# Reordering the row dots and the route scatters inside the expert stage of a hybrid decoder step

## The reference

```python
def peer_ffn(h, w_q, subkeys, u, v):
    q = (xt @ w_q).reshape(n, PEER_HEADS, 2, PEER_HALF)
    s = jnp.einsum('nhpd,hpkd->nhpk', q, subkeys)
    s_top, i_top = lax.top_k(s, PEER_TOPK)
    ...
    best, sel = lax.top_k(cand, PEER_TOPK)
    eidx = jnp.take_along_axis(cand_idx, sel, axis=-1)
    gate = jax.nn.softmax(best, axis=-1)
    ...
        a = jax.nn.gelu(jnp.einsum('ted,td->te', u[ib], xb))
        return jnp.einsum('te,ted->td', gb * a, v[ib])
```

## Time and profile before

| What | Value |
|---|---|
| Median of 3 runs | 4431.86 us (4416.49 to 4433.48) |
| The profiled execution, its own time | 4428.74 us |
| Its span, first to last instruction | 4427.1 us |
| Mean granted clock of TensorE | 0.972 |
| PE busy | 4207.2 us, 95% |
| DVE busy | 2647.8 us, 60% |
| POOL busy | 1483.2 us, 34% |
| First matmul of the stage of the change | 1943.7 us |
| Gathers and scatters issued | 2054.8 to 3276.0 us |
| Last dot begins | 3289.3 us |

### The profile page before, as it was taken

The page is one execution under the profiler, slowest core; times in us unless marked ns, Lnnn a source line. Parts: engine busy times, 40 slices in busy tenths (PEclk is TensorE's granted clock), DMA queues, the critical chain, the costliest instruction groups (busy, mean ns, idle before and its releaser), DMA issues. The chain is left out here.

```text
span 4427.1 us, 76388 instructions
## 1 busy us (share of the span) xinstructions
PE 4207.2 (95%) x28752; PEld 4110.5 (93%) x28752; DVE 2647.8 (60%) x3612; ACT 1246.2 (28%) x1625; POOL 1483.2 (34%) x1265
## 2 busy tenths in 40 slices
PE   6999999999897899979999999998889999999997
PEld 6999999999765899979999999998789999999997
DVE  5322211111222552245878999998679988888887
ACT  4211132333222221233332333232223223233232
POOL 1000000000011000001446666666736666566552
PEclk8999999999898999989999999999899999999998
DMA  5822333333477443235778887888899999999996
GB/s 209 309 78 85 111 113 109 105 102 107 158 285 268 150 141 123 70 130 179 257 268 280 292 289 282 300 310 302 314 378 368 357 364 355 361 357 359 360 354 256
DMA packets 282382, 1061.85 MB, mean 240 GB/s; under 512 B 43650, under 2 KB 94082, under 8 KB 228930
## 3 DMA queue, kind: packets, MB, share of 16 engines
q1 hardware_dynamic: 165042, 521.13, 33.4%
q0 software_dynamic: 90576, 499.53, 30.4%
q10 hardware_dynamic: 26624, 39.37, 2.4%
HBM read 977.47 MB, written 81.33 MB: 239 GB/s over the span
## 5 line engine op out<-in xcount | busy, mean ns | idle before, releaser
L145 DVE TENSOR_TENSOR w_lo<-w_raw,w_hi 128x1024 fp32r<-128x1024 f32 x458 | 550.9, 1230 | 840.9 <-ACT w_hi L136 840.7
L136 ACT ACTIVATE w_hi<-w_raw 128x1024 fp32r<-128x1024 f32 x458 | 476.3, 1058 | 1019.7 <-PE acc L173 566.4
L173 PE MATMUL acc<-x_hi,w_hi 128*128 128x288 f32 x2592 | 559.6, 298 | 13.3 <-DVE w_lo L145 9.3
L173 PE MATMUL acc<-x_lo,w_hi 128*128 128x288 f32 x2592 | 558.4, 297 | 0.0
L173 PE MATMUL acc<-x_hi,w_lo 128*128 128x288 f32 x2592 | 558.0, 297 | 0.0
L1572 POOL DMA_INDIRECT routes_scratch<-gate_sums,route x384 | 489.6, 1275 | 144.6 <-issue 115.5
L173 PEld LDWEIGHTS acc<-x_hi,w_hi 128*128 128x128 f32 x2592 | 420.7, 190 | 14.9 <-DVE w_lo L145 9.7
L173 PE MATMUL acc<-h_hi,w_hi_peeru 128*128 128x384 f32 (+1 forms) x1280 | 406.4, 334 | 23.5 <-DVE w_lo_peeru L145 23.5
L173 PEld LDWEIGHTS acc<-x_lo,w_hi 128*128 128x128 f32 x2592 | 420.6, 190 | 0.0
L173 PEld LDWEIGHTS acc<-x_hi,w_lo 128*128 128x128 f32 x2592 | 420.4, 190 | 0.0
L173 PE MATMUL acc<-h_hi,w_hi 128*128 128x384 f32 (+1 forms) x1280 | 401.1, 330 | 14.1 <-DVE w_lo L145 14.1
(11 more groups left out here) (340 smaller groups left out, 8302.1 us busy)
## 6 DMA issues: line engine op xcount, KB each, us to landing
w_raw<-in_w_peer_u SPq DMA_DIRECT2D x256, 512.0 KB, 5.2
w_raw<-in_w_peer_v SPq DMA_DIRECT2D x256, 512.0 KB, 6.5
w_raw<-in_w_gate SPq DMA_DIRECT2D x96, 512.0 KB, 3.6
w_raw<-in_w_z SPq DMA_DIRECT2D x66, 512.0 KB, 3.5
k_ring<-in_cache_k SPq DMA_DIRECT2D x64, 512.0 KB, 6.3
v_ring<-in_cache_v POOLq DMA_DIRECT2D x64, 512.0 KB, 6.9
routes_scratch<-zero POOLq DMA_DIRECT2D x8, 3072.0 KB, 46.4
activations_scratch<-a_out ACTq DMA_DIRECT2D x128, 192.0 KB
```

The costliest lines, as they stand in the source:

```text
L136: nc.scalar.activation(slot(q, j)[0], raw[:, j % 4, :], ACT.Copy).then_inc(q["hi"], 1)
L145: nc.vector.tensor_tensor(lo, raw[:, j % 4, :], hi.bitcast(F32), ALU.subtract).then_inc(q["lo"], 1)
L173: last = nc.tensor.matmul(dst, l_, r_[:, cc, c0:c0 + cn], start=(cc == first and p_ == 0), stop=(cc == last_c and p_ == 2))
```

## The change

It edits the two functions that lay out the order. No instruction is added or removed; gathers, scatters and dots change places among the stripes and among each other.

```diff
         def dots_by(s):
 
-            if s < 16:
-                return 0
-            return s - 15 if s <= 34 else min(NGAT, 19 + 7 * (min(s, LAST_FREE) - 34) // 5 + 11 * max(0, s - LAST_FREE) // 5)
+            if s <= 32:
+                return min(24, 3 * max(0, s - 13) // 2)
+            return min(NGAT, 24 + 7 * (min(s, LAST_FREE) - 32) // 5 + 11 * max(0, s - LAST_FREE) // 5)
 
         def scatters_before(q):
 
-            return min(NSCT, 9 * q // 4)
+            return min(NSCT, 9 * q // 4, 48 * (q // 24 + 1))
```

## The result

| | before | changed |
|---|---|---|
| Median | 4432.1 us (4 runs, 4416.5 to 4433.5) | 4528.4 us (4 runs, 4513.6 to 4534.7) |
| Profiled execution, its own time | 4428.7 us | 4534.7 us |

The ratio is 1.0218, 95% interval 1.0189 to 1.0247: **slower by 2.2%, 96 us**. The forecast was 4516 us, slower, with a range up to 4543. Of the 106 us between the two profiled executions, 5.7 lie ahead of the stage (its first matmul starts at 1949.5 us against 1943.7). The stage itself, from its first matmul to its last, grew from 1345.8 to 1445.7 us, by 99.9.

The account below looks back on a forecast made before the run. PE bounds the kernel, losing time where it waits for DVE's weight splits, late when POOL's gathers are. Stalls 109.7 plus slow starts 9.4 give +119, less 34 given back: +85 us on 4431.9, about 4516; range 4474 to 4543.

Parts of the forecast that it names:

- run of 18 (k = 3): 18 scatters in a row before a gather make PE wait for stripe 68: late by 7.1 us.
- run of 24 (k = 4): 24 scatters in a row, priced at 35.6 us, delay the split of stripe 86: late by 11.4 us.
- run of 30 (k = 5): 30 scatters in a row, priced at 42.6 us, delay a split that PE wants: late by 11.5 us.
- run of 36 (k = 6): 36 scatters in a row: PE late by 31.3 us, and 2 more while gathers 146 to 149 come 4.4 us apart.
- run of 42 (k = 7): 42 scatters in a row make PE wait for split 131: late by 46.4 us.
- slow starts: After each of five stalls PE starts at the low clock level, costing 1.9 us each, 9.4 us in all.
- gain in stripes 119 to 143: Outside the bursts, 25 stripes would run at 8.40 us each, 210.0 instead of 242.3 us: 32.3 us given back.
- Covered early runs: Rival, 12%: the bursts k = 3 to 5 cost nothing, as ring and lead hold more than counted: +49 us, 4481.
- A backlog behind a run: Rival, 10%: scatters hold up the gather behind them, so k = 3 to 7 cost 5.6 us more each: 4545 us.
- Free scatters: Rival, 5%: scatters issue so fast that the ring covers the bursts; only the gain of 34 us stays: 4398 us.
- Bursts and gain cancel: Rival, 3%: the bursts cost 34 us in all, as much as is given back: 4432 us.
- Early stripes overfull: Rival, 1%: the 20 us of dots added in stripes 14 to 28 are not hidden by DVE's idle time: 4536 us.

Follow-up runs that it names:

- the even spread: Changed kernel with each head's 48 scatters spread evenly over the gathers until the next head is ready, 1 a gather for the last: 4403.0 us, ratio 0.9940.

## Why the prediction was right

**The mechanism and its places** held: runs of 6 to 42 scatters before gathers 24 to 168, PE's waits at stripes 68, 86/87, 103, 120 and 131, the first two runs covered, no wait in stripes 15 to 32, none at 123 to 130, and 124.8 us of PE waits in the stage where I named "near 120". One sign that I had named for being wrong did show in part: after a run a row landed well under 7.8 us (see below).

**The terms.**

| Term | Forecast | Measured |
|---|---|---|
| run of 18 (k = 3) | 7.1 | 6.7 |
| run of 24 (k = 4) | 11.4 | 5.3 + 5.0 |
| run of 30 (k = 5) | 11.5 | 14.9 |
| run of 36 (k = 6) | 31.3 + 2 | 31.7 + 2.9 |
| run of 42 (k = 7) | 46.4 | 46.7 |
| sum | 109.7 | 113.3 |
| slow starts | 9.4, five stalls | 18.0, eight stalls, 1.4 to 3.1 each; 0.5 more at stripe 115 |
| gain in stripes 119 to 143 | -32.3 | -31.6: they take 299.0 us for 242.2, and 210.6 without the stalls and slow starts (210.0 in the even spread) |
| dot more at stripe 100 | 0 | +2.2 (2.81 for 0.65) |
| dot less at stripe 114 | 0 | -2.3 (8.75 for 11.01) |
| tail behind the last matmul | -2 | 0 |

The slow starts are read by laying the two traces over each other, matmul by matmul, and taking the stall from what each place adds. The measured terms give 113.3 + 18.5 - 31.6 + 2.2 - 2.3 = 100.1; the stage grew by 99.9. So what I missed of the time is the slow starts above all, 9 us. I had taken five where there are eight, each at the 1.9 us of one stall.

Three readings in the prediction are off and change little. Of the 22.7 us that "come after" the 11 us stall, 0.7 come before it, at stripe 101. The run of 24 is priced at 35.6 us; its own rule, 29 us at 1.50 and the rest at 1.28, gives 35.0. And with 1.28 us for every scatter the sum would be some 19 us less, not 14.

**Two errors inside a burst cancelled.** The chain took 7.8 us from a gather's issue to its landing, the median over all gathers. After the five runs even the dot began 5.6 to 6.0 us after the issue (3270.22 to 3275.81 above). The queue had then carried no row for 28 us and more, which is the likely reason; no run tests it by itself. And the runs were slower than I had them: from the first scatter to the gather 28.5, 37.9, 50.0, 51.9 and 56.9 us against 27, 35.6, 42.6, 49.6 and 56. That adds 14.4 us over the five, and the quicker rows take some 10 off: that the stalls came out within 4 us of the forecast is partly luck. The run of 30 is the mis-sized one. It falls on the sums of a head, of which the first two of three instructions have two SBUF inputs, 2.56 us each; under these a scatter takes up to 3.10 us. POOL's timeline of the changed kernel, then DVE's:

```profile
2895.22 3.10 POOL L1572 DMA_INDIRECT routes_scratch<-gate_sums,route  x1 [0.31 <-issue]
2898.62 2.29 POOL L1572 DMA_INDIRECT routes_scratch<-gate_sums,route  x1 [0.30 <-issue]
2901.22 0.97 POOL L1572 DMA_INDIRECT routes_scratch<-gate_sums,route  x1 [0.30 <-issue]
2902.49 0.96 POOL L1572 DMA_INDIRECT routes_scratch<-gate_sums,route  x1 [0.30 <-issue]
2903.76 2.58 POOL L1572 DMA_INDIRECT routes_scratch<-gate_sums,route  x1 [0.30 <-issue]
```

```profile
2894.92 2.55 DVE L1752 TENSOR_TENSOR same_expert<-eid_f,eidx 128x2304 f32<-128x2304 f32 x1
2897.51 2.56 DVE L1754 TENSOR_TENSOR same_expert<-same_expert,gate 128x2304 f32<-128x2304 f32 x1
2900.10 2.55 DVE L1756 TENSOR_REDUCE gate_sum_part<-same_expert 128x48 f32<-128x2304 f32 x1
2902.69 0.21 DVE L1757 TENSOR_TENSOR gate_sums<-gate_sums,gate_sum_part 128x48 f32<-128x48 f32 x1
2902.93 2.56 DVE L1752 TENSOR_TENSOR same_expert<-eid_f,eidx 128x2304 f32<-128x2304 f32 x1
```

The reduction has one input, and the two scatters under it run at 0.97.

**The stage's end.** I credited 2 us because DVE's last dot would no longer trail PE. It now starts at 3363.9 us, 31 us before PE's last matmul ends, yet from the stage's last matmul to the end of the program it is 1138 us in both traces. DVE's last dot wasn't what the end hung on. In both kernels ACT's first split of the next stage comes 3.7 to 3.9 us after ACT issued the store of the last stripe's activations (3290.13 to 3294.06 before, 3395.73 to 3399.39 changed), and ACT's last wait of the stage is for those stores.

**The rivals.** Covered early runs: out, 32 us of stalls there. A backlog behind a run: out, the rows landed sooner. Free scatters: out, 1.28 us each. Bursts and gain cancel: out, the stalls behind the runs alone are 113 us. Early stripes overfull: out, and the kernel with the new dots and no runs says so by itself.

**The Trainium skill.** The Trainium skill, DMA: Bandwidth & Descriptors, section Anatomy of one DMA, gave an estimate of 4.4 us for a row's landing. After a run, from issue to the dot, the trace shows 5.6, so the estimate is nearer to that than to the 7.8 of the median, and still short. The Trainium skill, SBUF — State Buffer, section Who interferes with whom, says that a DVE instruction with two SBUF inputs contends with a GpSimd instruction that reads SBUF. If the issue of a gather or scatter counts as one, the runs agree (1.46, 1.65 and 1.89 us a POOL instruction with none, a third and all of the dots of that kind).

## What to carry to other kernels

Where a cumulative schedule is cut off by a bound that rises in steps, print the differences between neighbours: a bound meant to hold back one head made arrears of up to 42 instructions for the later ones. On an in-order queue that carries urgent and idle work, a run of idle work costs its length less what the buffers behind it cover; spread it, and put as little of it as possible where the urgent work is densest. A weighted rate that just fits on average can still be short in one stretch, and the rate to reckon with is the one measured while the other engines work (here 1.51 us an instruction, not the 1.28 of an idle DVE).

## What the runs showed of the hardware

In the trace of before, 272 of the 576 gathers and scatters on POOL have no two-input DVE instruction (TENSOR_TENSOR or SCALAR_TENSOR_TENSOR with no input in PSUM) beside them. They took 0.98 us on average and none over 1.1. Of the 304 beside one, 189 were slow, and the 304 took 1.57 us on average. In the kernel with all dots from SBUF 440 lie beside one, 304 are slow, 1.75 us on average. What matters is what DVE is doing when the POOL instruction starts. All 189 and all 304 slow ones start under such a DVE instruction, and of those that do, 216 and 335, about nine in ten are slow. A POOL instruction that moves only four bytes per partition can so take 3.1 us.

And TensorE's slow start didn't grow with the stall. After 46.7 us of waiting, 12 matmuls ran at about 0.32 us apart, the lower of the clock's two levels, until the next began at 3287.51, as after 11.0 us in the earlier trace rows. After the stalls of 5.3 and 2.9 us it was 18 and 19 matmuls. Over the nine stalls of the changed kernel it was 10 to 19, in no order of the stall's length.
